# Three bf16 gate parts shared by GpSimd and ScalarE instead of two fp16 parts on VectorE, in the expert-routing build of a two-block network

## What is computed

```python
def peer_ffn(x, w_peer_q, peer_subkeys, peer_u, peer_v):
    ...                                     # top 16 of 128 x 128 experts, for each of 8 heads
    experts = i1 * N_KEYS + i2
    gates = jax.nn.softmax(best_s, axis=-1).astype(x.dtype)
    ...
    def chunk(args):
        xc, ec, gc = args
        u = peer_u[ec]
        act = jax.nn.gelu(jnp.einsum('tkd,td->tk', u, xc))
        return jnp.einsum('tk,tkd->td', gc * act, peer_v[ec])
```

## Time and profile before

| | us |
|---|---|
| median of 3 runs | 4225.85 |
| lowest and highest | 4199.53 and 4226.96 |
| the profiled execution, its own time | 4226.96 |
| span in its profile | 4225.2 |
| first build (r = 0), from TensorE's first L804 to the last `gated` | 69.12 |
| second build (r = 1), the same | 69.12 |

### The profile page before, as it was taken

One profiled execution on the slowest core, in us unless ns is written; L12 is line 12 of the kernel. 1 busy time (PEld: TensorE's weight loads), 2 busy tenths in 40 slices (PEclk: granted clock), 3 DMA queues, 4 the chain that ended last, 5 costly groups with the idle time before them and its releaser, 6 DMA issues.

```text
span 4225.2 us, 75507 instructions
## 1 busy us (share of the span) xinstructions
PE 3922.8 (93%) x30630; PEld 3733.5 (88%) x30630; DVE 1704.1 (40%) x2343; ACT 1484.1 (35%) x1771; POOL 2913.1 (69%) x1164
## 2 busy tenths in 40 slices
PE   9699997779998889999999899999999999999987
PEld 1599995779997887989999899999999999899986
DVE  0567347854213334264014288135443000644433
ACT  0112431233343333354443334422443443144442
POOL 0347980767785664868888779855887888288864
PEclk9799998889998999999999999988999999699997
DMA  9366650544442342534444445433554545154532
GB/s 349 116 245 263 261 218 20 218 159 153 168 179 105 142 158 80 185 144 169 186 175 177 150 174 184 180 138 111 187 188 170 183 185 188 62 187 186 182 135 96
DMA packets 98367, 713.79 MB, mean 169 GB/s; under 512 B 11040, under 2 KB 11168, under 8 KB 12064
## 3 DMA queue, kind: packets, MB, share of 16 engines
q1 hardware_dynamic: 97344, 705.75, 45.1%
q10 hardware_dynamic: 864, 5.76, 0.4%
HBM read 709.37 MB, written 2.10 MB: 168 GB/s over the span
## 4 chain that ended last, share of the span: by engine, by line
PE 78%; DVE 10%; POOL 6%; issue 4%; ACT 2%; DMA 1%; DVEq 0%; POOLq 0%; ACTq 0%; SPq 0%
PE bank L464 51%; PE bank L827 17%; POOL unit_lo L424 5%; PE bank L804 3%; PE bank L525 2%; PE bank L511 1%; DVE log_a L1721 1%; DVE rms_tmp L1586 1%; DMA ring<-in_w 1%; PE bank L617 1%; DVE y_attn L1707 1%; PE bank L599 1%; ACT att_s L999 0%; ACT unit_hi L851 0%; DVE rstd L1219 0%
## 5 line engine op out<-in xcount | busy, mean ns | idle before, releaser
L424 POOL TENSOR_TENSOR unit_lo<-ring,unit_hi 128x1024 fp32r<-128x1024 f32 x1140 | 2862.8, 2527 | 1021.0 <-ACT unit_hi L851 1019.8
L464 PE MATMUL bank<-xl_hi,unit_hi 128*128 128x256 f32 x5696 | 1616.9, 284 | 143.2 <-POOL unit_lo L424 59.1
L851 ACT ACTIVATE unit_hi<-ring 128x1024 fp32r<-128x1024 f32 x1140 | 1173.5, 1055 | 1317.0 <-PE bank L464 533.3
L464 PE MATMUL bank<-xl_lo,unit_hi 128*128 128x256 f32 x5696 | 1605.0, 282 | 0.0
L464 PE MATMUL bank<-xl_hi,unit_lo 128*128 128x256 f32 x5696 | 1604.7, 282 | 0.0
L464 PEld LDWEIGHTS bank<-xl_hi,unit_hi 128*128 128x128 f32 x5696 | 1085.1, 191 | 158.0 <-issue 69.3
L464 PEld LDWEIGHTS bank<-xl_hi,unit_lo 128*128 128x128 f32 x5696 | 1085.2, 191 | 0.0
L464 PEld LDWEIGHTS bank<-xl_lo,unit_hi 128*128 128x128 f32 x5696 | 1084.3, 190 | 0.1
L827 PE MATMUL bank<-w_r,unit_hi 128*128 128x256 f32 x4096 | 727.8, 280 | 4.5 <-DVE w_r L1874 4.5
L827 PEld LDWEIGHTS bank<-w_r,unit_hi 128*128 128x128 f32 x4096 | 628.9, 188 | 5.0 <-issue 5.0
L827 PE MATMUL bank<-w_r,unit_lo 128*128 128x256 f32 x2048 | 574.2, 280 | 0.0
(11 more groups left out here) (361 smaller groups left out, 4275.8 us busy)
## 6 DMA issues: line engine op xcount, KB each, us to landing
ring<-in_w SPq DMA_DIRECT2D x671, 1024.0 KB, 4.8
resid<-in_xT ACTq DMA_DIRECT2D x1, 2048.0 KB, 12.9
tmp_ctx<-in_ctxT ACTq DMA_DIRECT2D x1, 2048.0 KB, 9.8
out<-resid SPq DMA_DIRECT2D x4, 512.0 KB, 2.6
con<-in_con ACTq DMA_DIRECT2D x1, 576.0 KB, 3.2
con<-in_con ACTq DMA_DIRECT2D x1, 448.0 KB, 6.3
p_tmp<-in_pT ACTq DMA_DIRECT2D x1, 256.0 KB, 3.3
vec<-in_vec ACTq DMA_DIRECT2D x1, 246.0 KB, 4.7
```

What stands on the lines that cost most here:

```text
L424: pool.tensor_tensor(lb[b][:], ring[slot][:, f * HALF:(f + 1) * HALF], hb[b][:].bitcast(F32), ALU.subtract).then_inc(lo_done, 1)
L464: mm = pe.matmul(bank[(s.t0 + tile[m]) % TILES][:, 0:T], w[b][:, (i % 8) * P:(i % 8 + 1) * P], mv[x][:, k, :], start=(k == 0 and w is hb a ...
L851: act.activation(hb[b][:], ring[slot][:, f * HALF:(f + 1) * HALF], ACT.Copy).then_inc(hi_done, 1)
```

## The change

The gate is split into three bf16 parts without scaling (before: two fp16 parts of the gate times 2^15). The one-hot matrices are bf16, with the tokens outermost. They are compared straight from the fp32 tables (`con` holds iota, `peer_gT` the indices and gates). The products with the gate parts leave VectorE: ScalarE makes part 0 with eight activations of 64 columns a group, with the gate as a scale read from memory; GpSimd makes parts 1 and 2 with one tensor_tensor each. TensorE runs three matmuls a token, 24 a group. `hot_g` becomes `hot_g0` (ScalarE) and `hot_g12` (GpSimd), and VectorE waits for both before it writes `oe` anew.

```diff
-        oa = [zone("hot1_0", 96, [P, NKEY, TG], F16), zone("hot1_1", 98, [P, NKEY, TG], F16)]
-        oe = [zone("hot2_0", 100, [P, I2, TG], F16), zone("hot2_1", 101, [P, I2, TG], F16)]
-        ob = [zone("hotg_0", 102, [P, 2, I2, TG], F16), zone("hotg_1", 104, [P, 2, I2, TG], F16)]
+        oa = [zone("hot1_0", 96, [P, TG, NKEY], BF16), zone("hot1_1", 98, [P, TG, NKEY], BF16)]
+        oe = [zone("hot2_0", 100, [P, TG, I2], BF16), zone("hot2_1", 101, [P, TG, I2], BF16)]
+        ob = [zone("hotg_0", 102, [P, 3, TG, I2], BF16), zone("hotg_1", 105, [P, 3, TG, I2], BF16)]
...
+                    if s.name in ("peer_u0", "peer_u1"):
+
+                        pool.wait_ge(S("gate_parts"), 1)
+                        with pool.Fori(0, T // TG // 2) as it:
+                            for k in range(2):
+                                before = int(s.name[-1]) * (T // TG) + k + 1
+                                pool.wait_ge(S("hot_2"), before + it * 2)
+                                pool.wait_ge(S("g_done"), before + it * 2)
+                                for x in (1, 2):
+                                    ins = pool.tensor_tensor(
+                                        ob[k][:, x], oe[k][:], gb[:, x, bass.ds(it * (2 * TG) + k * TG, TG)].unsqueeze(2)
+                                        .to_broadcast([P, TG, I2]), ALU.mult)
+                                ins.then_inc(S("hot_g12"), 1)
...
-                        pe.wait_ge(S("hot_g"), i + 1)
+                        pe.wait_ge(S("hot_g0"), i + 1)
+                        pe.wait_ge(S("hot_g12"), i + 1)
                         pe.wait_ge(S("g_used"), i + 1)
                         for t in range(TG):
-                            for x in range(2):
-                                mm = pe.matmul(bank[5 + k][:, t * I2:(t + 1) * I2], oa[k][:, :, t], ob[k][:, x, :, t],
-                                               start=(x == 0), stop=(x == 1), skip_group_check=True)
+                            for x in range(3):
+                                mm = pe.matmul(bank[5 + k][:, t * I2:(t + 1) * I2], oa[k][:, t, :], ob[k][:, x, t, :],
+                                               start=(x == 0), stop=(x == 2), skip_group_check=True)
...
+                act.wait_ge(S("gate_parts"), 1)
+
+                def gate_part(it, r=r):
+
+                    for k in range(2):
+                        i = r * (T // TG) + k + it * 2
+                        act.wait_ge(S("hot_2"), i + 1)
+                        act.wait_ge(S("g_done"), i + 1)
+                        for t in range(TG):
+                            ins = act.activation(ob[k][:, 0, t, :], oe[k][:, t, :], ACT.Copy,
+                                                 scale=gT[:, 2:3, bass.ds(it * (2 * TG) + (k * TG + t), 1)]
+                                                 .rearrange("p a t -> p (a t)"))
+                        ins.then_inc(S("hot_g0"), 1)
+                with act.Fori(0, T // TG // 2) as it:
+                    gate_part(it)
...
-                    dve.tensor_tensor(oe[k][:], places[:, r * I2:(r + 1) * I2, :],
-                                      bc(picked[:, 1, bass.ds(i * TG, TG)], I2), ALU.is_equal).then_inc(S("hot_2"), 1)
+                    dve.tensor_tensor(oe[k][:], bc(C("iota", r * I2, (r + 1) * I2), TG),
+                                      gT[:, 1, bass.ds(i * TG, TG)].unsqueeze(2).to_broadcast([P, TG, I2]),
+                                      ALU.is_equal).then_inc(S("hot_2"), 1)
...
-                    dve.tensor_tensor(oa[k][:], places[:], bc(picked[:, 0, bass.ds(i * TG, TG)], NKEY), ALU.is_equal
-                                      ).then_inc(S("hot_1"), 1)
-
-                def hot_parts(i, k, r=r):
-
-                    dve.wait_ge(S("hot_2"), r * groups + 1 + i)
-                    dve.tensor_tensor(ob[k][:], oe[k][:].unsqueeze(1).to_broadcast([P, 2, I2, TG]),
-                                      gb[:, :, bass.ds(i * TG, TG)].unsqueeze(2).to_broadcast([P, 2, I2, TG]), ALU.mult
-                                      ).then_inc(S("hot_g"), 1)
+                    dve.tensor_tensor(oa[k][:], bc(C("iota"), TG), gT[:, 0, bass.ds(i * TG, TG)].unsqueeze(2)
+                                      .to_broadcast([P, TG, NKEY]), ALU.is_equal).then_inc(S("hot_1"), 1)
...
-                    dve.scalar_tensor_tensor(w_, bank[5 + k][:, :].rearrange("p (t i) -> p i t", t=TG), 1.0 / GATE_UP,
-                                             w_, ALU.mult, ALU.mult).then_inc(S("g_used"), 1)
+                    dve.tensor_tensor(w_, w_, bank[5 + k][:, :].rearrange("p (t i) -> p i t", t=TG), ALU.mult
+                                      ).then_inc(S("g_used"), 1)
...
+                        dve.wait_ge(S("hot_g0"), r * groups + k + 1 + it * 2)
+                        dve.wait_ge(S("hot_g12"), r * groups + k + 1 + it * 2)
                         hot_2(i + 2, k)
                         gated(i, k)
                         hot_1(i + 2, k)
-                        hot_parts(i + 2, k)
```

More of the change, by code:

```diff
@@ L27 @@
 U32 = mybir.dt.uint32
-F16 = mybir.dt.float16
+BF16 = mybir.dt.bfloat16
 ALU = mybir.AluOpType
@@ L56 @@
 BIG = 3.0e38
-GATE_UP = 2.0 ** 15
 SCALE = 192.0 ** -0.5
@@ L315, in program @@
         gT = zone("peer_gT", 113, [P, 3, T])
-        oa = [zone("hot1_0", 96, [P, NKEY, TG], F16), zone("hot1_1", 98, [P, NKEY, TG], F16)]
-        oe = [zone("hot2_0", 100, [P, I2, TG], F16), zone("hot2_1", 101, [P, I2, TG], F16)]
-        ob = [zone("hotg_0", 102, [P, 2, I2, TG], F16), zone("hotg_1", 104, [P, 2, I2, TG], F16)]
-        places = nc.alloc_sbuf_tensor_at("places", [P, NKEY, TG], F16, offset=z0 + 116 * KB)
-        picked = nc.alloc_sbuf_tensor_at("picked", [P, 2, T], F16, offset=z0 + 112 * KB)
-        gb = nc.alloc_sbuf_tensor_at("gate_parts", [P, 2, T], F16, offset=z0 + 110 * KB)
+        oa = [zone("hot1_0", 96, [P, TG, NKEY], BF16), zone("hot1_1", 98, [P, TG, NKEY], BF16)]
+        oe = [zone("hot2_0", 100, [P, TG, I2], BF16), zone("hot2_1", 101, [P, TG, I2], BF16)]
+        ob = [zone("hotg_0", 102, [P, 3, TG, I2], BF16), zone("hotg_1", 105, [P, 3, TG, I2], BF16)]
+        gb = zone("gate_parts", 109.5, [P, 3, T], BF16)
         gres = zone("gate_rest", 111, [P, T])
@@ L1818, in _ @@
             gate = gT[:, 2, :]
-            go(dve.tensor_scalar(gate, gate, GATE_UP, None, ALU.mult)); sync()
             go(dve.tensor_copy(gb[:, 0, :], gate)); sync()
@@ L1822, in _ @@
             go(dve.tensor_copy(gb[:, 1, :], gres[:]))
-            go(dve.tensor_copy(picked[:], gT[:, 0:2, :]))
-            go(dve.tensor_copy(places[:], C("iota").unsqueeze(2).to_broadcast([P, NKEY, TG])))
+            go(dve.tensor_copy(gate, gb[:, 0, :])); sync()
+            go(dve.tensor_tensor(gres[:], gres[:], gb[:, 1, :], ALU.subtract)); sync()
+            go(dve.tensor_copy(gb[:, 2, :], gres[:]))
             event("gate_parts")
@@ L1854, in _ @@
                     hot_1(k, k)
-                    hot_parts(k, k)
                 dve.wait_ge(tile_free["A"], TILES + PLAN[f"peer_v{r}"].ta)
```

## The result

The change makes the kernel slower: 4316.5 us median of 4 runs (4307.5 to 4324.33) beside 4218.56 us, median of 4 runs, for the kernel before; the ratio is 1.0239, with a 95% interval from 1.0211 to 1.0266. The profiled execution took 4325.57 us with a span of 4323.8, which is 98.6 us more than the span before. Forecast were 4365 us and 3.3%: the direction and the mechanism held, but the loss was forecast two fifths too large (138 us for 98.6).

The account below looks back on a forecast made before the run. The prediction took VectorE to bound the builds at 2.13 us a group. Four instructions in turn plus a signal made 4.31 us, 68.8 us more a build, 138 us for both: 4365 us, range 4280 to 4450 us.

Parts of the forecast that it names:

- What bounds the build before: In the two builds, VectorE sets the pace at 2.13 us a group, with TensorE at 88%.
- The turns: In the build, VectorE's two comparisons and GpSimd's two products exclude each other, one instruction each: 4.31 us a group; chance 0.62.
- The forecast signs: In the profile: builds near 138 us, TensorE busy about half, comparisons of 1.2 to 2.4 us, GpSimd with hardly a gap.
- The term that was mis-sized: GpSimd's product of 512 elements in the build, priced from one of 1024: 1.24 us, so 2.48 us a group.
- The narrower range: Whole-kernel time of 4330 to 4430 us, given for turns with a product between 1.0 and 1.7 us.
- TensorE's step: 24 matmuls a group in the build at the old 0.117 us each: 2.81 us, 3.07 with the gap between groups.
- VectorE, ScalarE, start: In the build: comparisons 0.60 and 1.13 us, part 0 1.9 us a group, TensorE starting 2.55 us after `peer_u`.
- TensorE binds: Rival: no exclusion or short products, so TensorE's 3.07 us paces the build; 4291 us; chance 0.17, ScalarE binding included.
- The dearer product: Rival: GpSimd's bf16 product in the build costs as much as 1024 fp32 elements; 6.61 us a group, 4502 us; chance 0.14.
- Not slower: Rival: contiguous weights and a 2.4 GHz clock speed TensorE in the build; 4261 us; chance 0.05 within 1%, 0.02 faster.
- By it the layout alone would give TensorE nothing: Inference for the build's matmuls from the skill's rule that 128 non-fp32 weight columns load faster, packed or strided alike.

Follow-up runs that it names:

- e8: Kernel before with 24 matmuls a group instead of 16 (part 1 added twice, so the computation is changed): 4274.64 us, one run.
- e1: Changed kernel with the iota row that both comparisons read moved to PSUM: 4230.85 us, ratio 1.0046 to the kernel before.
- e10: Kernel before with contiguous `hot_2` from PSUM iota, `hot_1` ahead of `gated`, ScalarE making seven tokens of part 0, GpSimd the eighth and part 1: 4203.86 us, ratio 0.9965.
- e7: Kernel before, its fp16 tables and comparisons kept, with gate part 0 made by ScalarE and part 1 by GpSimd: 4245.03 us, ratio 1.0073.

## Why the prediction was right, and where its sizes were off

*What bounds the build before.* VectorE, at 2.13 us. e8 confirms it from the other side: eight matmuls more, 0.94 us at the measured price, raise the group by only 0.77, the rest being TensorE's slack.

*The turns.* Shown by e1. The forecast signs in the profile came: comparisons of 1.5 and 1.8 us, the pair of products longer by 0.98 us through `hot_1`, VectorE's wait inside its instructions. Three came weaker than written: a build is 116 us in the windows and not 138, TensorE is busy for 40% and not half, and GpSimd keeps one gap a group, 0.72 us in which it waits for the stretched `hot_2`. Two of the readings behind this step were loose, though the conclusion held. The 0.888 us of L1253 is the mean of 32, most of which didn't wait (median 0.426, highest 2.612); what parts it from L1741 is that L1741 never takes more than 0.427. And of the operations of 2.90 and 2.63 us in `peer_u0` the second is `hot_2`, which costs 0.42 elsewhere and not 0.69. The prediction has each instruction hold the port for its whole length. That comes out to about 0.14 us a turn while the writes are contiguous, and not where the write is slow (the run with the weights strided).

*The term that was mis-sized* is "Half the elements: (2.385 - 0.10) / 2 + 0.10 = 1.24 us". A product costs 1.04 us, and 1.00 from start to start in a row. That is 0.48 us a group, of 0.56 by which 4.31 exceeds 3.75. The rest, 0.08 us a group, is what the turns overlap beyond the tails that the sum takes off (0.41 us and 0.26), less the 0.07 by which the signal to GpSimd is longer (0.17 us for 0.10). A build was forecast to lose 68.8 us and loses 50.6. Of the 18.2 between them, 29 periods make 16.2, the start 1.5 and the tail 1.4, and the late `peer_v` takes 0.9 back. With 18.6 in the second build that is 36.8 of the 39 us by which I was too high. The other 2.2 lie ahead of the end of the first `peer_u`; no run says whether they come from the change.

The median of 4316.5 us lies in the stated range, but below the narrower one from 4330 to 4430 us, which I gave for turns with a product between 1.0 and 1.7 us. The product is in that band and the time isn't: with 1.00 us the sum gives 3.83 us a group and 4336 us, still 10 above the profiled execution, which lies 9 above the median in turn. The narrower range was too high at its lower end.

*TensorE's step* "the value I take is the old pace" was wrong by a factor of two (1.31 for 2.81 us). In the steady loop that cost nothing, as TensorE is hidden in either case. At the start the products of group 2 begin 4.3 us behind `peer_u` (2818.89) and not 5.45, and the tail behind the last product is shorter by 1.4 us.

*VectorE, ScalarE, start.* 0.60 and 1.13 us for the comparisons (e1: 0.60 and 1.14), 2.01 us for part 0 against 1.9, the first matmul 2.6 us behind `peer_u` against 2.55. All right.

*The rivals.* "TensorE binds" fell with 3.75 us and a TensorE busy for 40%. The dearer product fell with 1.04. "Not slower" was right that the new layout makes TensorE fast, but gave it to the weights (it is the moving operand, by the two runs on strides), and its clock didn't rise (0.50); the reasoning that this can't help while the turns stand held. "By it the layout alone would give TensorE nothing" took a rule on weights for one on the whole layout.

## What to carry to other kernels

Before work is moved from VectorE to GpSimd, look where its neighbours read: in these runs an instruction of VectorE with two SBUF inputs and a product of GpSimd took turns, and the wait showed as a longer instruction, not as idle time. One shared operand in PSUM removed it (e1). The two-input instruction placed before the product gave the wait to GpSimd, 0.28 us of it, which helps where GpSimd has time (e10). And a layout has a price on each side: here fast fp16 comparisons want the tokens inside and fast matmuls want the moving operand contiguous, so choose by which engine is the bound, and choose for each operand apart.

## What the runs showed of the hardware that was not expected

- A matmul of 64 columns whose moving operand steps by 16 bytes costs 0.112 us, contiguous 0.055 (24 in 2.69 and 1.31 us), at the same clock of 0.50. The weights' stride is worth 0.009.
- Writing bf16 at a stride of 16 bytes costs VectorE 3.5 us more for 1024 elements (4.55 instead of 1.09 behind the product it waits for). GpSimd needs 2.49 us at the least instead of 1.04 for 512, ScalarE 0.58 at the least (median 0.76) instead of 0.33 for 64. ScalarE reading at that stride: 0.402 for 0.332.
- GpSimd's product of 512 bf16 or fp16 elements is 1.04 us, under half of the 2.385 us of `unit_lo` for 1024 in fp32.
- Whether VectorE or GpSimd waits goes by which is issued first: `hot_1` in e7 (1.08 for 0.68 us), the product in e10 (1.32 for 1.04).
- The second of two instructions in turn can begin before a slow strided write of the first is through (0.41 us behind it for a product of 1.04).
